# Feed-forward of a decoder step in two phases: gate and up by seven products over two token blocks, h to device memory, then down in rounds of four tiles

## The reference

```python
D_MODEL = 1024; SEQ = 1024; D_FF = 2816          # 22 tiles of 128
def _swiglu(x, w_gate, w_up, w_down):
    return (jax.nn.silu(x @ w_gate) * (x @ w_up)) @ w_down

x = _layer_norm(DN_ALPHA * x + 0.5 * _swiglu(x, f1g, f1u, f1d), ln_g[0], ln_b[0])   # FFN1
m, s_new, new_k, new_v = _mixer(x, w_in, w_out, gn_w, sinks, ...)                   # retention and attention
x = _layer_norm(DN_ALPHA * x + m, ln_g[1], ln_b[1])
x = _layer_norm(DN_ALPHA * x + 0.5 * _swiglu(x, f2g, f2u, f2d), ln_g[2], ln_b[2])   # FFN2
```

## Time and profile before

| | us |
|---|---|
| median of three runs | 2095.16 |
| span of the profiled execution | 2093.6 |
| FFN1 from its first multiplication to the end of its last down product | 6.5 to 785.8 |
| FFN2 likewise | 1310.2 to 2081.2 |
| PE busy | 2053.0 (98%) |
| DVE busy | 1147.6 (55%) |
| POOL busy | 721.3 (34%) |
| ACT busy | 552.2 (26%) |

### The profile page before, as it was taken

The page is one execution under the profiler, slowest core; times in us unless marked ns, Lnnn a source line. Parts: engine busy times, 40 slices in busy tenths (PEclk is TensorE's granted clock), DMA queues, the critical chain, the costliest instruction groups (busy, mean ns, idle before and its releaser), DMA issues.

```text
span 2093.6 us, 31226 instructions
## 1 busy us (share of the span) xinstructions
PE 2053.0 (98%) x11749; PEld 1886.0 (90%) x11749; DVE 1147.6 (55%) x2046; ACT 552.2 (26%) x947; POOL 721.3 (34%) x421
## 2 busy tenths in 40 slices
PE   8999999999999999999998999999999999999997
PEld 8999999999999889999797667999999999999986
DVE  4655665566555752111556636266556655665566
ACT  3222122202220262121146444222202221222125
POOL 3331343234323352221453423243324332434133
PEclk9999999999999999999999999999999999999999
DMA  6111011111111022110124011111111111011112
GB/s 253 41 41 60 23 57 40 60 40 40 40 60 40 21 111 86 41 50 28 49 93 149 1 51 36 61 41 55 45 43 37 60 40 59 21 60 40 60 41 86
DMA packets 38074, 118.39 MB, mean 57 GB/s; under 512 B 6271, under 2 KB 10879, under 8 KB 37759
## 3 DMA queue, kind: packets, MB, share of 16 engines
q1 hardware_dynamic: 38015, 117.58, 16.1%
HBM read 106.29 MB, written 11.27 MB: 56 GB/s over the span
## 4 chain that ended last, share of the span: by engine, by line
PE 94%; DVE 3%; issue 1%; ACT 1%; DMA 1%; SPq 0%; DVEq 0%; ACTq 0%
PE bank L119 21%; PE bank L121 21%; PE bank L120 21%; PE bank L596 6%; PE bank L598 6%; PE bank L597 6%; PE bank L2093 2%; PE bank L2095 2%; PE bank L2094 2%; PE bank L2063 1%; PE bank L610 1%; PE bank L609 1%; PE bank L2013 1%; PE bank L986 1%; PE bank L1415 1%
## 5 line engine op out<-in xcount | busy, mean ns | idle before, releaser
L754 DVE TENSOR_TENSOR acc<-acc,bank 128x512 f32<-128x512 f32 x1000 | 623.9, 683 | 247.7 <-PE bank L598 233.3
L119 PE MATMUL bank<-x_hi,f_w_hi 128*128 128x362 f32 (+1 forms) x2104 | 689.5, 328 | 1.1 <-DVE x_low L162 1.1
L121 PE MATMUL bank<-x_hi,f_w_low 128*128 128x362 f32 (+1 forms) x2104 | 690.2, 328 | 0.0
L119 PEld LDWEIGHTS bank<-x_hi,f_w_hi 128*128 128x128 f32 x2104 | 395.5, 188 | 8.1 <-issue 1.4
L121 PEld LDWEIGHTS bank<-x_hi,f_w_low 128*128 128x128 f32 x2104 | 395.6, 188 | 0.0
L120 PE MATMUL bank<-x_lo,f_w_hi 128*128 128x362 f32 (+1 forms) x1056 | 346.1, 328 | 0.0
L120 PE MATMUL bank<-x_low,f_w_hi 128*128 128x362 f32 (+1 forms) x1048 | 343.6, 328 | 0.0
L479 POOL TENSOR_TENSOR f_w_low<-f_w_raw,f_w_hi 128x1024 fp32r<-128x1024 f32 x88 | 211.7, 2427 | 323.4 <-ACT f_w_hi L354 314.6
L364 ACT ACTIVATE f_h_full<-bank 128x362 f32<-128x362 f32 (+1 forms) x132 | 62.1, 471 | 904.2 <-PE bank L121 904.1
L707 DVE TENSOR_TENSOR f_h_full<-bank,f_h_full 128x362 f32<-128x362 f32 (+1 forms) x132 | 70.6, 535 | 337.4 <-PE bank L121 334.8
L497 POOL TENSOR_TENSOR f_ds_raw<-f_d_raw 128x512 f32<-128x512 f32 x60 | 77.1, 1299 | 378.8 <-DMA f_d_raw<-ffn_in 378.8
(11 more groups left out here) (252 smaller groups left out, 3094.3 us busy)
## 6 DMA issues: line engine op xcount, KB each, us to landing
f_w_raw<-ffn_in SPq DMA_DIRECT2D x88, 512.0 KB, 4.2
f_d_raw<-ffn_in SPq DMA_DIRECT2D x44, 512.0 KB, 4.2
rp_w_raw<-w_ret_in SPq DMA_DIRECT2D x16, 512.0 KB, 3.6
acc<-x_rows_in SPq DMA_DIRECT2D x2, 2048.0 KB, 10.9
kept_rows<-acc SPq DMA_DIRECT2D x8, 512.0 KB, 2.6
ow_raw<-w_out_in SPq DMA_DIRECT2D x8, 512.0 KB, 7.0
y_out<-acc SPq DMA_DIRECT2D x8, 512.0 KB, 2.6
n_rows<-ln_rows_in SPq DMA_DIRECT2D x6, 512.0 KB, 5.6
```

The costliest lines, as they stand in the source:

```text
L119: pe.matmul(out, wh, xh, start=first, stop=False)
L121: return pe.matmul(out, wl, xh, start=False, stop=last)
L754: x = dve.tensor_tensor(acc[:, t, d], acc[:, t, d], down_ps[n % 4][:, :], op)
```

## The change

The new `ffn_stage` has two phases.

**Phase 1**, for all 22 tiles: two blocks of 384 tokens (C0, C1) and a rest of 320 (C2). For the two blocks, gate and up over the two halves of k are a 2x2 block product and are done with seven products of four k (`product`, 12 multiplications of 384 columns each); the rest is done plainly (G2 and U2, 24 multiplications of 320 columns each). A tile is 84 + 48 = 132 multiplications. Four sums of weights (`sum_tile`, L932 to L937) are made by DVE for the next tile, ACT rounds them, POOL makes their low parts (`split_sums`). For the blocks, x needs four sums beside x itself, which are made once, at the start of each feed-forward (`vector_sums` in FFN1; in FFN2 `Norm.low`, `Norm.fourth` and `extra_low`). h is stored to device memory, 557 KB a tile.

**Phase 2**: 20 tiles in five rounds of four. A round is one 2x2 block product in which each block is two tiles deep: seven products of 4 x 2 x 3 multiplications and two decode groups of 8, 184 multiplications of 512 columns, added up over the two tiles in PSUM. h and the down weights of a round are loaded (4.3 MB), summed and split: h by DVE (`left_sum`, `low_left`), the weights by POOL (`right_sum`, `low_right`). DVE reads the products 30 times a round (`read`). P1 and P6 go to a shared sum and not to `acc`, and are merged in the last round. The residual rows are loaded into `acc` only at the start of phase 2 and scaled in the first read. Tiles 20 and 21 are done as before, without a gate and up chunk among them.

```diff
+    STEADY = ("P1", "P6", "P7", "P2", "P4", "P5", "G2", "P3", "U2")
+    OPENING = ("P1", "P2", "G2", "U2", "P5", "P7", "P6", "P4", "P3")
+    Q_ORDER = ("P1", "P2", "D0", "P5", "P3", "P6", "P7", "D1", "P4")
...
+    def split_tile(pool, f, s, j):
+        pool.wait_ge(*past(gu_hi, 4 * f + j + 1))
+        if j == UP or not (isinstance(f, int) and f == 0):
+            pool.wait_ge(*past(sums_done, 4 * f + 4))
...
+    def right_sum(pool, q, name):
...
+        if name == "T1":
+            pool.wait_ge(*past(draw_in[q % 2], 32 * (q // 2) + 32))
+            if q:
+                pool.wait_ge(*past(*downed(q - 1, "P5")))
...
+        elif name == "T2":
+            if q:
+                pool.wait_ge(*past(*downed(q - 1, "P6")))
+            x = pool.tensor_tensor(out, b22, b_.right(q, "T1")[0], SUB)
...
+    def bank_free(pe, q, name, t):
+
+        if name == "P1":
+            if q:
+                pe.wait_ge(*past(*read_of(q - 1, "P4", t)))
...
+            pe.wait_ge(*past(*read_of(q, {"P2": "P1", "P3": "P5", "P6": "P2", "P7": "P6", "P4": "P7"}[name], t)))
...
+    def sum_tile(dve, f, s, use):
+
+        for j in range(2):
+            dve.wait_ge(*past(staged[s][j], 16 * (use + 1)))
...
+        dve.tensor_tensor(s1, a21, a22, ADD).then_inc(sums_done, 1)
+        dve.tensor_tensor(s3, a11, a21, SUB).then_inc(sums_done, 1)
+        dve.wait_ge(*past(sums_done, 4 * f + 1))
+        dve.tensor_tensor(s2, s1, a11, SUB).then_inc(sums_done, 1)
+        dve.wait_ge(*past(sums_done, 4 * f + 3))
+        dve.tensor_tensor(s4, a12, s2, SUB).then_inc(sums_done, 1)
...
+    def down_vector(dve):
...
+        for q in range(ROUNDS):
+            more = q + 1 < ROUNDS
+            read(dve, q, "P1")
+            if q == 0:
+                left_sum(dve, 0, "S1")
+                left_sum(dve, 0, "S3")
+                left_sum(dve, 0, "S2")
+                left_sum(dve, 0, "S4")
+            decode_low(dve, q)
+            low_left(dve, q, "S1")
+            read(dve, q, "P2")
+            read(dve, q, "D0")
+            low_left(dve, q, "S4")
+            low_left(dve, q, "S2")
+            read(dve, q, "P5")
+            low_left(dve, q, "S3")
+            low_left(dve, q, "A22")
+            if more:
+                left_sum(dve, q + 1, "S1")
+            read(dve, q, "P3")
+            if more:
+                left_sum(dve, q + 1, "S3")
+            read(dve, q, "P6")
+            if more:
+                left_sum(dve, q + 1, "S2")
+                left_sum(dve, q + 1, "S4")
...
+            read(dve, q, "P7")
+            read(dve, q, "D1")
+            if more:
+                low_left(dve, q + 1, "A11")
+                low_left(dve, q + 1, "A12")
+                decode_sum(dve, q + 1)
...
+            read(dve, q, "P4")
```

More of the change, by code:

```diff
@@ L121, in three_passes @@
     return pe.matmul(out, wl, xh, start=False, stop=last)
-def load_stage(core, x_in, x_tok_in, small_in, small, eps, eps_twice, acc, xh, x_raw, xl):
-    sem = lambda n: core.semaphore("load_" + n)
[L127 to L135, removed]
+FFN_CHUNKS = [(0, 384), (384, 768), (768, TOK)]
@@ new lines, in pairs, with weights_of, gate_raw, downed @@
+    def pairs(eng, step):
+        with eng.Fori(1, FT // 2 - 1) as q:
+            step(2 * q, 0, q)
+            step(2 * q + 1, 1, q)
+    def weights_of(f, j, n=1):
+        if isinstance(f, int):
+            return w_in[f, :, j, :]
+        return w_in[bass.ds(f, 1), :, j, :].rearrange("a p n -> (a p) n")
+    def gate_raw(f, s):
+        return b_.gate0 if isinstance(f, int) and f == 0 else b_.w_raw[s][GATE]
+    def downed(q, name, t=None):
+        n = FIRST_OF[name] + (t if t is not None else 0 if name in ("D0", "D1") else 3)
+        return down_done, PER_ROUND * q + n + 1
@@ new lines, in down_bank, with group @@
+    def down_bank(name, t):
+        return core.banks[{"D0": 7, "D1": 4}[name] if name in ("D0", "D1") else 4 + t if name in ("P5", "P3") else t]
+    def group(pe, q, name):
+        left, right = PRODUCTS[name]
+        pe.wait_ge(*past(left_lo, len(LEFT_LO) * q + LEFT_LO.index(left) + 1))
+        pe.wait_ge(*past(right_lo, len(RIGHT_LO) * q + RIGHT_LO.index(right) + 1))
+        h_hi, h_lo = b_.hi[left], b_.left(q, left)[1]
+        w_h, w_l = b_.hi[right], b_.right(q, right)[1]
+        first = name not in MORE
+        for t in range(4):
+            bank_free(pe, q, name, t)
+            out, m = down_bank(name, t)[:, :], slice(P * t, P * t + P)
+            for g in range(2):
+                pe.matmul(out, h_hi[:, g, m], w_h[:, g, :], start=first and g == 0, stop=False, skip_group_check=not first)
+                pe.matmul(out, h_lo[:, g, m], w_h[:, g, :], start=False, stop=False, skip_group_check=not first)
+                mm = pe.matmul(out, h_hi[:, g, m], w_l[:, g, :], start=False, stop=g == 1, skip_group_check=not first)
+            mm.then_inc(down_done, 1)
@@ new lines, in decode @@
+    def decode(pe, q, name):
+        bank_free(pe, q, name, 0)
+        pe.wait_ge(*past(dec_lo, 3 * q + 4))
+        out = down_bank(name, 0)[:, :]
+        parts = ((0, "B11"), (2, "B21")) if name == "D0" else ((4, "B22"), (0, "T3"))
+        for n, (pack, right) in enumerate(parts):
+            pe.wait_ge(*past(right_lo, len(RIGHT_LO) * q + RIGHT_LO.index(right) + 1))
+            w_h, w_l = b_.hi[right], b_.right(q, right)[1]
+            for g in range(2):
+                pe.matmul(out, b_.packs[:, pack + g, :], w_h[:, g, :], start=n == 0 and g == 0, stop=False)
+                mm = pe.matmul(out, b_.packs[:, pack + g, :], w_l[:, g, :], start=False, stop=n == 1 and g == 1)
+        mm.then_inc(down_done, 1)
@@ L2407, in decoder_layer @@
[L2407 to L2416 removed]
+    pack = Layout(nc, mix_end + 8192).put("op_pack", [P, KT * P + DEC], F32R)
```

1573 lines of the change are left out of this document (901 added, 672 removed).

## The result

The changed kernel takes 2151.47 us (median of 4 runs, 2150.95 to 2151.88); the kernel before, beside it, 2095.43. The ratio is 1.027, 95% interval 1.0256 to 1.0285: 2.7% slower. The profiled execution has a span of 2149.5 us, 55.9 more than before's 2093.6. Forecast were 2146 us and a span 50.4 longer.

A forecast was written before the change was run, and what follows sets the result against it. PE, busy 98% of the span, was taken as the bound. The span 2093.6 - 88 + 30 + 108 + 0.4 = 2144, plus 1.6 for the runs' median, gave 2146 us; 8-in-10 range 2070 to 2172.

The forecast's parts named there:

- gate and up, 42 tiles: Phase 1, tiles after the first: fewer multiplications save 2.1 us a tile, -88 us in all; bounds -53 to -90.
- the first tiles: Start of each feed-forward: extra sums and low parts delay tile 0, +14 and +16 us, together +30; bounds +12 to +45.
- down: Phase 2: DVE and POOL exclude each other and delay rounds, +54 us a feed-forward, +108; bounds 0 to +154.
- tails: Last two tiles' down products: norm 1's chain barer, +1 us in FFN1, -0.6 in FFN2; together 0 to +8.
- The bound at which 320 columns cost as much as 362: Phase 1: if the shorter multiplications went no faster, 0.8 us a tile would be lost, leaving -53.
- The estimate of -80: Gate and up by the skill page's back-to-back formula: a tile goes from 22.1 to 20.2 us.
- The mechanism and its place: End of a down round: DVE and POOL take turns ahead of P4's read, so P1 waits; PE stands 6.5 us.
- their rivals: Down, in the follow-ups: shared SBUF bandwidth; total exclusive work, rounds 51; DVE's late list, rounds 55 and more; no chances given.
- The clock's 1.7: Down rounds starting behind a PE gap: granted clock falls to 0.50 for 3.3 us, half lost, +1.7 us each.
- the bound of 8: Tails: upper end of the range 0 to +8 us for both feed-forwards together.
- One reason in the text: Kernel before, down part: DVE's two-operand instructions never met POOL because POOL waited for them by `h_ready`.

The follow-up runs named there:

- e1: Separate test, not the layer: DVE and POOL instructions alone and side by side; DVE's with two SBUF operands took 1.22 us alone, 3.36 beside POOL.
- e3: Changed kernel with one low part of h and the decode sum moved behind DVE's read of P4; span 2111.6 us against 2149.5.
- e5: Changed kernel with all of POOL's phase 2 sums and low parts issued by DVE; span 2129.7 us against 2149.5.
- e11: Changed kernel with 20 unread identity multiplications on PE behind P4 of each round but the last; span 2131.9 us against 2149.5.
- e7: Kernel before the change, without POOL's wait for `h_ready` in the down weights; span 2093.3 us against 2093.6.
- e10: Changed kernel with the down weights' sums on DVE, DVE's phase 2 order rearranged, and the norm's transpositions one token tile later; 2080.58 us.

## Why the prediction was right, by its steps

Where each term ended, in spans, with the changed kernel's profile against before's (a tile 24.0, the down part 210.5, from the earlier trace rows):

| term | forecast | measured |
|---|---|---|
| gate and up, 42 tiles | -88 | -95.3 (21 x 2.20 and 21 x 2.34) |
| the first tiles | +30 | +31.4 (13.8 and 17.6) |
| down | +108 | +108.9 (53.3 and 55.6) |
| tails | +0.4 | +8.0 (7.1 and 0.9) |
| between the feed-forwards | 0 | +2.9 |
| sum | +50.4 | +55.9 (span: +55.9) |

The first tiles are what is left of phase 1, 499.8 and 499.2 us from its first multiplication, after 21 tiles of 21.80 and 21.66: 42.0 and 44.3 us. FFN1's is counted from the start of the span, 50.3 us against 36.5, since PE also starts 1.8 us later (8.3 us, before 6.5); FFN2's was 26.7 us before. The tails are what is left behind the last round: 41.9 us in FFN1 against 34.8, and to the end of the span 43.1 against 42.2. How a pair's 69.05 us of before divide into gate, up and down is the prediction's reckoning; 0.1 us more or less a tile would move 4 us between the first and the third row, and nothing in the sum.

The forecast of the span was 5.5 us too low, and that is a sum of misses of both signs: gate and up gained 7.3 us more than forecast, the tails cost 7.6 more, and the other rows 1 to 3 each. That the total is so close is in part luck.

**Gate and up.** Right, slightly undersized: 21.80 and 21.66 us a tile, not 21.93. The bound at which 320 columns cost as much as 362 is out. The estimate of -80, worked out from the Trainium skill ("TensorE: Matmul & The Clock Gate", Back-to-back issue gap), is further off than the rows'; the page gives that formula for an isolated multiplication.

**The first tiles.** In FFN1 the sum was right (50.4 forecast, 50.3 measured), and its parts nearly: behind the last load two of DVE's instructions of 1536 elements (L295, L297) took 3.9 and 3.8 us in turns with POOL and the others 1.76, DVE had done its share of x at 39.4 us where 41.0 were reckoned, and its own first products then took longer than reckoned (L963 2.3 and L971 2.6 us). FFN2's first tile took 44.3 us from its first multiplication where 42.3 were forecast.

**Down.** The mechanism and its place were right, and e1, e3, e5 show them apart from their rivals: turns (e1), at the queue ahead of a read that frees P1's bank (e3), gone with POOL (e5). ACT, the loads and DVE's own load are excluded by e3 and e5, where all three are as before or more. The sizes fit less well one by one than in sum. Rounds 1 to 3 were 51.0 where 52.1 was forecast: the turns from T2 on took 18.6 us (655.95 to 674.57) instead of 19.1, since a pair of turns is 3.28 us (e1) and not 3.56, and they began 31.4 us into the round, reckoned were 30.2 and the clock's 1.7. Round 0 was 65.9 and 67.7 where 64 was forecast: D0 waited 7.5 us and not 9, but P7 6.7 and not 3.3, and half clock cost about 5 us in it and not 3.4. Round 4 was 45.3 where 44.0 was forecast. So the 108 came out also because these cancel. The clock's 1.7 us was the right size (1.5 to 2, e11), though the rows that it was read from show 3.1 us of work at half clock and not 3.3.

**Tails.** The term that was missed: +7.1 in FFN1 where +1 was taken, and +8.0 in all, at the bound of 8. The gate and up chunk that stood among the last down products had filled the norm's start. PE's waits in the tail, after and before:

```profile
PE bank L1258 <- DVE acc L1246: 5.2, 1, 5.2
PE bank L1258 <- DVE x_low L1286: 1.9, 2, 1.3
```

```profile
PE bank L986 <- DVE x_low L1004: 1.2, 1, 1.2
```

They explain 5.9 of the 7.1 us. The granted clock in the tail was 0.96 where it was 1.00 before, which can be worth up to 1.7 us; that part was not tested by itself.

**One reason in the text was incomplete**, without an effect on the sum: that DVE's and POOL's work never met before was put down to POOL's wait for `h_ready`. e7 shows that this wait did nothing: ACT's rounding held POOL back, and ACT itself waits there for `h_ready`.

**Open.** What adds 2.9 us between the feed-forwards (0.7 to 1.9 in the other runs of the new structure, e10 aside) was not tried.
